# The first eight weight sums of a hybrid decoder block: from VectorE additions to accumulating DMAs, with the first two pairs reordered

## What is computed

```python
h = rms_norm(z, norm_w)                     # 1040 x 1024
p = h @ w_in + b_in                         # w_in: 1024 x 8192
q, fz, iv, g_hg, u, g_pool, m_hg, m_pool = split(p)
lb = cumsum(softmax(lb_logits))             # lower bounds of the forget gates
log_f = log(lb + (1 - lb) * sigmoid(fz));  k = (1 - lb) * sigmoid(-fz)
o = hgrn2_chunkwise(q, k, iv, log_f)        # 8 heads, gated linear recurrence
y_hg = (rms_norm(o) * silu(g_hg)) @ w_down_hg
y_pool = (mix(pool(u)) * silu(g_pool)) @ w_down_pool
z = z + (sigmoid(m_hg) * y_hg + sigmoid(m_pool) * y_pool) @ w_out
return rms_norm(z, final_norm_w)[16:]
```

## Time and profile before

| | us |
|---|---|
| median of 3 runs | 1072.56 |
| lowest and highest | 1071.41, 1073.38 |
| the profiled execution, its own time | 1072.64 |
| its span, first to last instruction | 1070.9 |
| PE busy in the span | 1035.6 (97%) |
| DVE busy | 777.6 (73%) |
| ACT busy | 491.0 (46%) |
| POOL busy | 98.0 (9%) |

### The profile page before, as it was taken

How to read it: one execution, slowest core, us unless ns; L and a number is a source line. 1 busy time by engine, 2 the same in 40 slices (tenths; PEclk the granted TensorE clock), 3 DMA queues, 4 the chain that set the end, 5 groups by cost and what they waited for, 6 DMA issues and landing times. The chain is left out here.

```text
span 1070.9 us, 18826 instructions
## 1 busy us (share of the span) xinstructions
PE 1035.6 (97%) x7444; PEld 847.3 (79%) x7444; DVE 777.6 (73%) x1245; ACT 491.0 (46%) x829; POOL 98.0 (9%) x164
## 2 busy tenths in 40 slices
PE   7889999999999999999999999999999999999995
PEld 6668888888888888878888888788887787787884
DVE  7887686868686868686676777774579689978133
ACT  7664535454535454544443533444457346345122
POOL 2500010101010101010101010011100110001111
PEclk9999999999999999999999999999999999999998
DMA  7022020202020201121312122127322764555232
GB/s 260 1 79 80 21 80 21 81 21 80 21 80 22 69 31 65 37 81 69 97 42 89 60 89 79 69 100 283 127 80 98 268 243 157 181 173 177 69 126 100
DMA packets 36055, 104.61 MB, mean 98 GB/s; under 512 B 4576, under 2 KB 4576, under 8 KB 35968
## 3 DMA queue, kind: packets, MB, share of 16 engines
q1 hardware_dynamic: 22064, 65.61, 18.5%
q0 software_dynamic: 8240, 26.79, 6.7%
q10 hardware_dynamic: 5664, 11.02, 2.8%
HBM read 78.23 MB, written 25.17 MB: 97 GB/s over the span
## 5 line engine op out<-in xcount | busy, mean ns | idle before, releaser
L1149 PE MATMUL acc<-r_hi,w_hi 128*128 128x512 f32 x1112 | 445.5, 401 | 14.1 <-DVE w_lo L1518 5.7
L1149 PE MATMUL acc<-r_hi,w_lo 128*128 128x512 f32 x1112 | 434.2, 390 | 0.0
L1149 PE MATMUL acc<-r_lo,w_hi 128*128 128x512 f32 x1112 | 433.7, 390 | 0.0
L1149 PEld LDWEIGHTS acc<-r_hi,w_hi 128*128 128x128 f32 x1112 | 208.8, 188 | 67.1 <-issue 19.8
L1149 PEld LDWEIGHTS acc<-r_hi,w_lo 128*128 128x128 f32 x1112 | 208.7, 188 | 45.0
L1149 PEld LDWEIGHTS acc<-r_lo,w_hi 128*128 128x128 f32 x1112 | 209.1, 188 | 39.9
L680 ACT ACTIVATE w_hi<-sum 128x512 fp32r<-128x512 f32 x156 | 98.0, 629 | 165.4 <-DVE sum L1554 83.4
L1518 DVE TENSOR_TENSOR w_lo<-sum,w_hi 128x512 fp32r<-128x512 f32 x156 | 106.6, 687 | 57.1 <-ACT w_hi L680 56.7
L1518 DVE TENSOR_TENSOR w_lo<-raw,w_hi 128x512 fp32r<-128x512 f32 x120 | 82.2, 688 | 64.7 <-ACT w_hi L680 64.7
L680 ACT ACTIVATE w_hi<-raw 128x512 fp32r<-128x512 f32 x120 | 74.7, 625 | 26.8 <-PE acc L1149 26.8
L1149 PE MATMUL acc<-wo_hi,m_hi 128*128 128x512 f32 x128 | 49.9, 390 | 0.6 <-DVE wo_lo L2192 0.6
(11 more groups left out here) (287 smaller groups left out, 1377.2 us busy)
## 6 DMA issues: line engine op xcount, KB each, us to landing
raw<-in_wstream SPq DMA_DIRECT2D x88, 512.0 KB, 3.7
xin<-in_x SPq DMA_DIRECT2D x8, 512.0 KB, 6.2
a_spill<-gt POOLq DMA_DIRECT2D x16, 256.0 KB, 3.6
c_spill<-pg POOLq DMA_DIRECT2D x16, 256.0 KB, 2.7
stage<-a_spill ACTq DMA_DIRECT2D x4, 1024.0 KB, 13.1
smh_spill<-zq POOLq DMA_DIRECT2D x16, 256.0 KB, 2.6
gate_in<-smh_spill SPq DMA_DIRECT2D x16, 256.0 KB, 5.2
part_spill<-zq POOLq DMA_DIRECT2D x16, 256.0 KB, 4.9
```

The costliest lines, as they stand in the source:

```text
L1149: ins = pe.matmul(out_ap, a, b, start=first and n == 0, stop=final and n == 2, skip_group_check=partial)
```

## The change

The four sums of pair 0 and of pair 1 are no longer made by DVE. SP first loads a21 three times, into the places of S1, S2 and S4 (`begin_sums`, 768 KB with one DMA), and once into the place of S3 (`begin_third`, 256 KB). POOL then issues DMAs that add to what lies there (`accum_op=ALU.add`): `grow_sums(p, 1)` adds a22 to all three (768 KB), `grow_sums(p, 2)` adds a11 to S2 and S4 (512 KB), `grow_sums(p, 3)` adds a12 to S4 (256 KB). Each waits for the one before it of the same pair. `make_third(p)` adds a11 to S3 (256 KB). All of them read the weights from DRAM. The tile `raw_early` and its load go away, and SP's reload of `raw0` no longer waits for sums.

On POOL these DMAs stand among the powers and behind most of the mask work, which moves forward between the powers. The small computation of the lower bounds (lb) moves to the front on DVE and ACT. V5 is split into two halves. The orders of DVE and ACT over the first two pairs are rewritten; so is the place of the transposes on PE. `first_low` is cut into `b11_low`, `b11_copy` and `b21_low`, and product (0,0) waits only for the first of them.

```diff
-S1, S2, S3, S4 = range(4)
+S1, S2, S4, S3 = range(4)
 SUM_OF = {2: S2, 3: S1, 4: S3, 5: S4}
...
+EARLY_SUM_AT = {S1: 1, S2: 2, S4: 3}
...
-ADD_ORDER = [(0, 11), (1, 11), (0, 12), (0, 22), (1, 12), (1, 22)]
+ADD_ORDER = [(0, 11), (0, 22), (1, 11), (0, 12), (1, 22), (1, 12)]
...
-                        sp.wait_ge(S["sums_made"], 4 * max(p + 1, EARLY))
+                        if p >= EARLY:
+                            sp.wait_ge(S["sums_made"], 4 * (p - EARLY + 1))
...
+            def begin_sums(p):
+
+                if p:
+                    sp.wait_ge(S["h_row"], 8)
+                sp.dma_start(sums_all[p][:, 0:3, :], wstream[2 * p + 1][:, 0:HALF].rearrange("p (o n) -> p o n", o=1)
+                             .to_broadcast([P, 3, HALF])).then_inc(sum_begun[p], 16)
+
+            def begin_third(p):
+
+                if p:
+                    sp.wait_ge(S["h_row"], CHUNKS + 1)
+                sp.dma_start(sums_all[p][:, S3, :], wstream[2 * p + 1][:, 0:HALF]).then_inc(third_begun[p], 16)
...
             load_x(6)
             load_x(7)
+            begin_sums(0)
+            load_x(8)
+            begin_third(0)
             load_raw(1)
-            sp.dma_start(raw_early[:, :], wstream[3]).then_inc(S["early_loaded"], 16)
-            load_x(8)
+            begin_sums(1)
+            begin_third(1)
+
             def load_gate(u):
 
...
+            def grow_sums(p, n):
+
+                first_one = n - 1
+                if n == 1:
+                    pool.wait_ge(sum_begun[p], 16)
+                else:
+                    pool.wait_ge(sum_grown[p], 16 * (n - 1))
+                block, half = ((1, 1), (0, 0), (0, 1))[n - 1]
+                src = wstream[2 * p + block][:, half * HALF:(half + 1) * HALF].rearrange("p (o n) -> p o n", o=1)
+                pool.dma_start(sums_all[p][:, first_one:3, :], src.to_broadcast([P, 3 - first_one, HALF]),
+                               accum_op=ALU.add).then_inc(sum_grown[p], 16)
+
+            def make_third(p):
+                pool.wait_ge(third_begun[p], 16)
+                pool.dma_start(sums_all[p][:, S3, :], wstream[2 * p][:, 0:HALF], accum_op=ALU.add) \
+                    .then_inc(third_made[p], 16)
...
+            x_rstd(6)
+            grow_sums(0, 1)
+            x_rstd(7)
+            grow_sums(0, 2)
+            x_rstd(8)
+            grow_sums(0, 3)
+            for n in range(1, 4):
+                grow_sums(1, n)
+            make_third(0)
+            make_third(1)
+            spread_masks()
...
             meta_copy(0)
             high(4)
             copy_first(1)
-            v5_high()
             high(5)
+            v5_high(0)
+            copy_early_fifth(0)
+            v5_high(1)
+            high(6)
             act.activation(o_ms[:, 0:1], minus_half[:, 0:1], ACT.Sigmoid)
-            copy_early_fifth(0)
-            high(6)
+            high(7)
             copy_early_fifth(1)
             v6_high(0)
             v6_high(1)
-            high(7)
             high(8)
             high(9)
             v7_high(0)
+            copy_second(0)
             v7_high(1)
-            copy_second(0)
             high(10)
             meta_place(0, 0)
+            high(11)
             copy_second(1)
             v4_high(0)
             v4_high(1)
-            high(11)
+            high(12)
+            high(13)
             act.wait_ge(S["lb_made"], 1)
             gates(0)
-            high(12)
-            high(13)
+            high(14)
+            high(15)
             prepare_copies(0)
             last_quarter(0)
-            high(14)
-            high(15)
             extra(1, 1)
             meta_place(0, 1)
...
+            low(4)
+            v5_sum(6)
+            low(5)
+            v5_sum(7)
+            v5_sum(8)
+            v5_low(0)
+            low(6)
+            v5_low(1)
             v6_sum(0)
             v6_sum(1)
             low(7)
             v6_low(0)
+            low(8)
             v6_low(1)
-            early_fifth(0)
-            low(8)
             low(9)
             v7_sum(0)
             v7_sum(1)
-            early_third_sum(0)
-            early_third_sum(1)
             v7_low(0)
+            low(10)
             v7_low(1)
-            low(10)
             v4_sum(0)
+            low(11)
             v4_sum(1)
-            add_12(0)
-            low(11)
+            early_fifth(0)
+            v4_low(0)
             add_22(0)
-            v4_low(0)
             v4_low(1)
             low(12)
+            add_11(1)
+            add_12(0)
             early_fifth(1)
+            add_22(1)
+            low(13)
             add_12(1)
-            low(13)
-            add_22(1)
+            low(14)
             dve.wait_ge(S["masks_spread"], 1)
             prepare(0)
-            low(14)
             low(15)
             weight_sums(2)
             low(16)
```

More of the change, by code:

```diff
@@ L222, in hybrid_block @@
         sums_at = here[0]
-        sums = [at(f"sum{n}", [P, HALF], F32) for n in range(4)]
+        sums_of = at("sums", [P, 4, HALF], F32)
+        sums = [sums_of[:, n, :] for n in range(4)]
         snaps_at = here[0]
@@ L553, in _, with x_rstd @@
                 pool.dma_start(dst, src).then_inc(S["params_loaded"], 16)
-            for i in range(CHUNKS + 1):
+            def x_rstd(i):
                 rows = META if i == 0 else P
@@ L559, in _, with runs @@
                                    ALU.pow).then_inc(S["x_rstd"], 1)
-            steps.mark(pool.memset(mask1[:, :, :], 1.0))
+            level0 = mask1[:, 0:2, :].rearrange("p a (b j) -> p (a b) j", j=2)
+            odd = mask1[:, 3, :]
+            def runs(m, n):
+                return mask1[:, n, :].rearrange("p (b j) -> p b j", j=1 << m)
             def keep(mask, base, channel, pattern):
@@ L566, in keep, with keep_from, keep_to, spread_masks @@
                                               pattern=pattern, channel_multiplier=channel))
[L568 to L571, removed]
+            def keep_from(m, n, lo):
+                keep(runs(m, n), -lo, 1, [[-(2 << m), 64 >> m], [0, 1 << m]])
+            def keep_to(m, n, hi):
+                keep(runs(m, n), hi, -1, [[2 << m, 64 >> m], [0, 1 << m]])
+            def spread_masks():
+                steps.settle()
+                pool.wait_ge(S["x_rstd"], CHUNKS + 1)
+                whole = mask1[:, 0:2, :].rearrange("p a t -> p (a t)")
+                for g in range(GROUPS):
+                    rows = slice(g * GROUP, (g + 1) * GROUP)
+                    pool.tensor_copy(mask[rows, 0, :], whole[rows, rows])
+                    ins = pool.tensor_copy(mask[rows, 2:MASKS, 0:16], mask1[rows, 2:MASKS, g * 16:(g + 1) * 16])
+                ins.then_inc(S["masks_spread"], 1)
+            def grow_sums(p, n):
[12 more added lines that the diff above has]
+                    .then_inc(third_made[p], 16)
+            x_rstd(0)
+            steps.mark(pool.memset(mask1[:, :, :], 1.0))
             steps.settle()
@@ L574, in _ @@
             keep(odd, -1, 1, [[-2, 64]])
-            for m, view, lo, _ in halves:
-                keep(view, -lo, 1, [[-(2 << m), 64 >> m], [0, 1 << m]])
+            x_rstd(1)
+            keep_from(1, 2, 0)
+            keep_from(2, 4, 0)
+            x_rstd(2)
+            keep_from(3, 5, 4)
+            keep_from(3, 6, 0)
+            x_rstd(3)
+            keep_from(4, 7, 0)
             steps.settle()
@@ L579, in _ @@
             keep(odd, 1, -1, [[2, 64]])
[L580 to L589, removed]
+            x_rstd(4)
+            keep_to(1, 2, 1)
+            keep_to(2, 4, 3)
+            x_rstd(5)
+            keep_to(3, 5, 7)
+            keep_to(3, 6, 3)
+            keep_to(4, 7, 15)
+            x_rstd(6)
[9 more added lines that the diff above has]
+            spread_masks()
             def o_rstd(r):
@@ L949, in _ @@
             square_x(3)
+            act.wait_ge(S["lb_shifted"], 1)
+            act.activation(lexp[:, :, :], lexp[:, :, :], ACT.Exp).then_inc(S["lb_exp"], 1)
             first_tile(1)
@@ L956, in _ @@
             first_tile(4)
+            high(1)
             square_x(6)
-            high(1)
             square_x(7)
-            act.wait_ge(S["lb_shifted"], 1)
-            act.activation(lexp[:, :, :], lexp[:, :, :], ACT.Exp).then_inc(S["lb_exp"], 1)
             square_x(8)
@@ L1355, in _ @@
             product(0, 0)
+            half(0, 1, 0)
             h_transposes(5)
-            half(0, 1, 0)
+            half(0, 1, 1)
             h_transposes(6)
-            half(0, 1, 1)
+            half(1, 0, 0)
             h_transposes(7)
-            product(1, 0)
+            half(1, 0, 1)
             h_transposes(8)
@@ L1519, in low @@
                     .then_inc(S["w_lo"], 1)
[L1521 to L1542, removed]
             def weight_sums(p):
@@ L1858, in _ @@
             dve.tensor_scalar(one_minus_lb[:, :], lb[:, :], -1.0, 1.0, ALU.mult, ALU.add).then_inc(S["lb_made"], 1)
+            b11_low(1)
+            b11_copy(1)
```

(33 more changed lines are left out.)

105 lines of the change are left out of this document (43 added, 62 removed).

## The result

| | before | after |
|---|---|---|
| median, us | 1072.14 (4 runs) | 1089.17 (4 runs, 1088.7 to 1089.67) |
| ratio to before, 95% interval | | 1.0158 (1.0146 to 1.0170) |
| span of the profiled execution | 1070.9 | 1087.0 |
| operand 5: its high part begins | 42.34 | 58.22 |
| event E, second half of product (2,0) | 82.17 | 99.22 |

The change costs 17.0 us by the medians, and 16.1 between the two executions that were profiled. The forecast was 1083.1 with a range of 1071 to 1094. The first line of the page of the changed kernel: PE is busy for 4 us more than in the earlier trace rows, with as many matmuls, so some of them ran slowly; DVE is busy for 5.6 us less, about what the eight sums took.

A forecast was written before the change was run, and what follows sets the result against it. PE, busy for 97% of the span, was taken as the bound. The sum for operand 5 at 52.05 plus 39.0, less 82.17, gave 8.9, with the clock 10.5; on a median of 1072.56: 1083.1 us, range 1071 to 1094.

The forecast's parts named there:

- Where the time is lost: Before product (1,5): operand 5's sum lands at 52.05, where its high part had begun at 42.34 in the kernel before.
- the sign that I had named: PE idle before (1,5) for some 9 us, released through w_hi and w_lo by a DMA into the sums.
- The start: Product (0,0) starts about 1.3 us earlier, which does not last, for PE soon needs the sums.
- nothing lost: Power of tile 8, queued behind grow_sums(0, 2), ends at 33.0; (1,1) starts at 36.3 against 36.15: nothing lost, nothing gained.
- The chain of DMAs: Five accumulating landings in series on POOL before operand 5, issued from 25.2: 25.9 us with doubled movement, best figures.
- From t5 to E: From operand 5's sum to the second half of (2,0): 39.0 us, plus 1.6 for the lower clock.
- t5: The time when operand 5's sum lands, forecast at 25.2 + 25.9 + 0.95 = 52.05 us.
- The sum: 52.05 + 39.0 = 91.05, less 82.17, is 8.9 us later; with the clock 10.5.
- The doubled case: The forecast's own case: adding doubles the DMAs' movement cost, by best or median figures, 1081 to 1087; chance 0.54.
- Plain cost: Rival: an accumulating DMA costs what a plain one does, 1074 to 1078; chance 0.17.
- Faster: Rival: sums are never late and DVE's shorter list shows, 1067.5 to 1069; chance 0.13.
- Four times the cost: Rival: movement of the accumulating DMAs costs four times, the five taking 41.3 us, 1098.5 in all; chance 0.16.

The follow-up runs named there:

- e5_dve: The changed kernel with its eight sums made by DVE again, raw_early and its load back, the rest of the new order kept: 1070.54 us, ratio 0.9990.
- e3_power: The changed kernel with the power of tile 8 issued on POOL before grow_sums(0, 2): 1091.01 us, ratio 1.0172.
- e1_plain: The changed kernel with plain instead of adding DMAs in grow_sums and make_third, same sizes and waits, sums incomplete: 1080.52 us.
- e8_plain_small: The changed kernel with each grow_sums writing S4 alone (256 KB) and all its DMAs plain, sums incomplete: 1076.78 us.
- e5b_dve_tail: As e5_dve, with last_quarter(0) also moved ahead of prepare_copies(0) on ACT: 1066.87 us, ratio 0.9953 to the kernel before.
- e2_small: The changed kernel with each grow_sums adding to S4 alone, 256 KB each, sums incomplete: 1082.13 us.
- e7_late_reload: The changed kernel with SP reloading raw0 only after the last growing DMA has landed: 1089.03 us.

## Why the prediction was right, point by point

**Where the time is lost.** Right. PE is idle before (1,5) for 11.87 us (I said about 9), released through w_lo and w_hi by a DMA into the sums. This was the sign that I had named, and the experiments bear the cause out: with the sums on DVE the loss is gone (e5_dve).

**The start.** (0,0) began at 21.66, 1.4 us earlier than before (I said 1.3), and it brought nothing. The power of tile 6 ended at 25.5 (I said 25.2). The power of tile 8 ended at 34.95 instead of 33.0, and product (1,1) started at 38.22 instead of 36.3, and at the lower clock. I had called this part "nothing lost"; it was 2 us late and slow. It did not count, since (0,5) waited for its sum anyway: in e3_power, without this stall, E came no earlier.

**The chain of DMAs.** The mechanism was right: five landings in series and one issue. The size of the term was too small. I took 25.9 us for the five; they took 32.1. Adding was nearly right: 7.7 forecast (25.9 less 18.2), 8.3 measured. The plain cost beneath it was the mis-sized term: 18.2 forecast, 23.8 measured in e1_plain. I had taken the best landing of quiet transfers and drawn it on by 0.7 us for each 256 KB. Measured against e8_plain_small, 256 KB more cost about 1.0. With the last step (3.05), the fourth (4.06) and the first (5.24) of e1_plain as the figures for 256, 512 and 768 KB, the five come to 21.6 by my estimate. The other 2.1 lie in the second and third step. What I called quiet was not: SP's loads stood beside the second, and `grow_sums(0, 3)` beside the third. With the median of 3.2 in the earlier trace rows, and 4.0 for 512 KB, the sum is 20.8 plain and 29.6 doubled, nearer, but only by 2.6 of the missing 5.6 us. POOL's loads with rows of 2 KB also moved at 331 GB/s, SP's with 4 KB at 407; whether the rows or the issuing engine make the difference was not tried.

**From t5 to E.** I walked 39.0 us and added 1.6 for the clock: 40.6. It was 41.0, and 40.6 to 41.4 in five other runs with the same ACT order. That (2,0) would wait for `last_quarter(0)`, not for its low part, came true: its row names ACT vt. The slow matmuls behind (1,5), which I had called covered by DVE, were perhaps not wholly so: the matmul that waits 1.48 us for r_lo begins 19.7 us after t5 in the changed kernel and 19.1 in e5_dve, which had none.

**The sum.** t5 0.3 late at the start, 5.85 in the chain, 0.4 behind it: E moved by 17.05 where I had 10.5. The doubled case, which I gave 0.54, ended at 1087; that 1089.2 still lies in the range is owed to the room left for DMAs of four times the plain cost, not to the sum.

**The rivals.** Plain cost (1074 to 1078) fell, and e1_plain shows that even without the adding the version takes 1080.5. Faster fell: it needed 17.0 us for the chain, and even e8_plain_small, neither adding nor large, took 19.1 for the five. With the sums on DVE t5 was 40.2, a little later than the 38.1 that this rival had reckoned for sums that are never late, and the gain was real once ACT's order was mended (e5b_dve_tail). Four times the cost fell: 41.3 against 32.1.

## What to carry to other kernels

Work that is moved from a busy engine to DMAs is not free where it stands on a chain: count the landings in series, each at its place in the trace with what runs beside it, and compare the sum with the time at which the first result is needed. The adding DMAs here moved their bytes at about half the rate of plain ones. When queues are rewritten by hand, look for what stands behind a waiting instruction on each engine; two swapped lines on ACT were worth 4 us here, nearly the 5.3 that taking all eight sums from DVE could have brought.

## What the runs showed of the hardware

An accumulating DMA into SBUF moved 172 GB/s at full busy share, the same DMA without adding 331, loads of 4 KB rows 407. Adding hardly occupies POOL longer: from the start of the issue of 768 KB to POOL's next instruction it was 0.87 us adding and 0.84 plain, with 256 KB 0.61 and 0.59 (25.52 to 26.39 and 39.55 to 40.16 in the changed kernel, 25.59 to 26.43 and 35.51 to 36.10 in e1_plain). The durations in the rows are longer for the adding ones, 1.33 against 0.81, but they overlap the instruction behind.

The granted clock did not follow the length of a gap alone: after 3.55 us idle in the changed kernel the matmuls fell to the lower pace from 95.4 on, after 3.59 us idle at the same place in the profiled execution of e5_dve they did not. The five other runs with the DMAs and the same ACT order (e1_plain, e2_small, e3_power, e7_late_reload, e8_plain_small) all had slow matmuls behind gaps of 3.56 to 3.58 us there. They and the changed kernel had had PE idle for 4.0 us or longer before (1,5), some 35 us earlier; e5_dve never for more than 1.5 us after 30 us. But the ten executions of e5_dve, one and the same program, had granted clocks from 0.993 to 0.997, so the earlier gap need not be the reason. Why is open.
